# A sixteen-expert loop with its experts ranked by token count and narrower gate and up products for the smaller ones

## The reference, cut to what matters

```python
gprob = softmax(x @ w_rg + b_rg);  gp, gidx = top_k(gprob, 1)
elog_sel = (x @ w_re + b_re) of group gidx
ep, eidx = top_k(softmax(elog_sel), 2);  ep = ep / sum(ep)
combine = sum(one_hot(gidx * 4 + eidx, 16) * (gp * ep))
for wg, wu, wd, c in experts:                 # 1024x512, 1024x512, 512x1024
    acc += c[:, None] * ((silu(x @ wg) * (x @ wu)) @ wd)
y = rmsnorm(x + acc, final_g)
```

## Time and profile before

| what | us |
|---|---|
| median of 3 runs | 878.69 |
| the same, lowest and highest | 877.14, 885.36 |
| span of the profiled execution | 877.9 |
| start of the barrier's end between b2_all and b3_all, in the span | 427.3 |
| start of the first expert's first product | 431.9 |
| start of the second step | 460.8 |
| length of an undisturbed step | 26.84 |

### The profile page before, as it was taken

How to read it: one execution, slowest core, us unless ns; L and a number is a source line. 1 busy time by engine, 2 the same in 40 slices (tenths; PEclk the granted TensorE clock), 3 DMA queues, 4 the chain that set the end, 5 groups by cost and what they waited for, 6 DMA issues and landing times.

```text
span 877.9 us, 15841 instructions
## 1 busy us (share of the span) xinstructions
PE 845.3 (96%) x5828; PEld 749.4 (85%) x5828; DVE 526.8 (60%) x1237; ACT 383.5 (44%) x734; POOL 244.6 (28%) x272
## 2 busy tenths in 40 slices
PE   6999999999999999998899999999999999999993
PEld 5989879999988787775789988889988999888992
DVE  5537424657778435557585676656666656766573
ACT  7545303656367425544334434344343444433442
POOL 1000000000000110002045654447545555445472
PEclk9999999999999999999599999999999999999997
DMA  9121001102222182336188889978899887898871
GB/s 291 43 97 47 2 0 49 49 1 56 49 96 96 59 274 91 150 145 216 60 275 290 300 304 325 306 271 310 291 310 324 307 288 278 290 360 295 286 256 50
DMA packets 118505, 166.56 MB, mean 190 GB/s; under 512 B 17012, under 2 KB 95928, under 8 KB 118469
## 3 DMA queue, kind: packets, MB, share of 16 engines
q1 hardware_dynamic: 103109, 135.48, 45.7%
q0 software_dynamic: 15360, 30.59, 10.2%
HBM read 146.84 MB, written 41.17 MB: 214 GB/s over the span
## 4 chain that ended last, share of the span: by engine, by line
PE 47%; another core or an unknown queue 1%; ACT 1%; issue 1%; DVE 0%; POOL 0%; ACTq 0%; POOLq 0%
PE bank L1912 31%; PE bank L1922 4%; PE bank L1933 3%; PE bank L1924 3%; PE bank L1923 3%; PE bank L1900 2%; PE bank L1893 1%; ACT split L2012 1%; POOL out L1820 0%; PE bank L1905 0%; DVE wdlo L2116 0%; PE bank L1939 0%; DVE x L2188 0%; ACT hs L2014 0%
## 5 line engine op out<-in xcount | busy, mean ns | idle before, releaser
L1912 PE MATMUL bank<-big,ring 128*128 128x160 f32 x2048 | 286.1, 301 | 0.1
L1912 PEld LDWEIGHTS bank<-big,ring 128*128 128x128 f32 x2048 | 281.9, 191 | 1.4
L1836 POOL TENSOR_TENSOR hold_at<-ident 128x1 f32<-128x1 f32 x63 | 53.1, 842 | 175.3 <-DVE lists L2083 128.4
L2116 DVE TENSOR_TENSOR wdlo<-wdn,split 128x1024 fp32r<-128x1024 f32 x64 | 76.7, 1219 | 0.0
L2008 ACT ACTIVATE sg<-bank 128x160 f32<-128x160 f32 x64 | 19.5, 304 | 109.7 <-PE bank L1912 95.4
L2012 ACT CAST split<-wdn 128x1024 fp32r<-128x1024 f32 x64 | 64.9, 1039 | 0.0
L502 PE MATMUL bank<-split,ring_r 128*128 128x384 f32 (+1 forms) x192 | 64.4, 336 | 0.1
L504 PE MATMUL bank<-split,ring_r 128*128 128x384 f32 (+1 forms) x192 | 61.7, 321 | 0.0
L2111 DVE TENSOR_TENSOR hs<-hid,hs 128x128 fp32r<-128x128 f32 x64 | 18.9, 295 | 57.3 <-ACT hs L2014 46.8
L1922 PE MATMUL bank<-split,hs 128*128 128x512 f32 x128 | 52.6, 411 | 0.0
L1399 PE MATMUL bank<-split,ring_r 128*128 128x512 f32 (+1 forms) x128 | 51.7, 404 | 0.3 <-PEq L1191 0.3
(11 more groups left out here) (390 smaller groups left out, 1788.4 us busy)
## 6 DMA issues: line engine op xcount, KB each, us to landing
wdn<-in_w_down SPq DMA_DIRECT2D x32, 1024.0 KB
ring<-in_w_gate SPq DMA_DIRECT2D x32, 1024.0 KB, 5.4
ring<-in_w_up SPq DMA_DIRECT2D x32, 1024.0 KB
ring<-in_w_in SPq DMA_DIRECT2D x8, 1024.0 KB, 5.9
x<-in_x_prompt SPq DMA_DIRECT2D x8, 512.0 KB, 6.1
h_rows<-h SPq DMA_DIRECT2D x8, 512.0 KB, 2.6
sums<-x SPq DMA_DIRECT2D x8, 512.0 KB, 3.6
v<-in_x_prompt SPq DMA_DIRECT2D x4, 512.0 KB, 5.4
```

Source lines behind the costliest of these rows:

```text
L1836: nc.gpsimd.tensor_tensor(hold_at[:], ident[:, 0:1], ident[:, 1:2], ALU.add).then_inc(e_hold, 1)
L1912: x = nc.tensor.matmul(bank[f % 2][:, side * 256:side * 256 + W], ring[:, u, k, c0:c0 + P], xT[:, k, :], start=k == 0, stop=k == KC - 1)
L2116: nc.vector.tensor_tensor(wdlo[:, k, :], wdn[:, k // 2, (k % 2) * D:(k % 2 + 1) * D], wdhi[:, k, :].bitcast(F32), ALU.subtract).then_inc(e ...
```

## The change

The weights' layout is not touched: before and after, gate and up are read in halves of 256 columns, runs of 1 KB. What changes:

- `order_experts`, new, on VectorE at the start of the first step (before, nothing stood there but the lists of step 0): expert 0 stays first, the other 15 are ranked by count, the smallest first. It writes the experts' order (`ids`), how much narrower than 160 the place of each expert is (`shift`), the number of steps (`steps`), and part 5 of the table, and raises the rank of tokens beyond the narrow width to the second round's. The counting of steps in b2_all (three operations and three more for `steps` and `once`), and GpSimd's making of part 5, go.
- Gate and up products are 132 columns wide in steps 1 to 6, 144 in steps 7 to 12, 160 in steps 0 and 13 to 15 (`WIDTHS`); TensorE's loop becomes three. Everything else stays at 160.
- Each engine reads the number of steps later: TensorE within step 0 behind f=1, ScalarE and VectorE behind step 0, GpSimd behind its first fetches. In every step SyncE and VectorE read the expert's number from `ids`.
- Within step 0, TensorE's list product moves from behind f=0 to behind f=1, and VectorE's third table from behind f=1 to behind f=2.
- Results have a list of their own, `lists_out`. GpSimd no longer waits for the results at the end of its pass; VectorE waits for the sums sent (e_sum) before it writes `lists_now`, and for the results of the step before (e_out) before it writes `lists_out`. At the end GpSimd waits once more, with a register load between.

```diff
+WIDTHS = [(1, 132), (7, 144), (13, W)]
...
-        link(nc.vector.tensor_reduce(mxc[:, 0:1], bank[6][:, 0:NE], axis=AX.X, op=ALU.max))
-        link(nc.vector.tensor_scalar(rlim[:, 0:ROUNDS], rlim[:, 0:ROUNDS], mxc[:, 0:1], float(NE), ALU.is_lt, ALU.mult))
-        link(nc.vector.tensor_reduce(mxc[:, 1:2], rlim[:, 0:ROUNDS], axis=AX.X, op=ALU.add))
+        nc.vector.tensor_copy(order.counts, bank[6][:, 0:NE])
...
+    def expert(eng, i):
+        return eng.value_load(ids[0:1, bass.ds(i, 1)], min_val=0, max_val=NE - 1)
+
     def count(eng):
+        eng.wait_ge(e_steps, 1)
         return eng.value_load(steps[0:1, 0:1], min_val=NE, max_val=NE * ROUNDS)
...
             pool.wait_ge(e_otl, i + 1)
+            pool.wait_ge(e_to, i + 1)
             hold()
             send_results(e_out)
-            pool.wait_ge(e_out, i * 64 + 64)
-            pool.sem_inc(e_free, 1)
...
         pool.wait_ge(e_fin, 64)
+        pool.wait_ge(e_out, last_step(pool) * 64)
...
-                x = nc.tensor.matmul(bank[f % 2][:, side * 256:side * 256 + W],
-                                     ring[:, u, k, c0:c0 + P], xT[:, k, :],
+                x = nc.tensor.matmul(bank[f % 2][:, side * 256:side * 256 + w],
+                                     ring[:, u, k, c0:c0 + P], xT[:, k, 0:w],
...
-                if first and f == 0:
+                if first and f == 1:
+                    ends.extend((count(pe), last_step(pe)))
                     pe.wait_ge(e_oh, 2)
                     pe.wait_ge(e_idx, 1)
                     indices(facts)
...
-        with pe.Fori(1, n - 1) as i:
-            step(i, False, False)
-        step(m, False, True)
+        for j, (a, w) in enumerate(WIDTHS):
+            with pe.Fori(a, WIDTHS[j + 1][0] if j + 1 < len(WIDTHS) else n - 1) as i:
+                step(i, False, False, w)
+        step(m, False, True, W)
...
+        def order_experts():
...
+            link(nc.vector.tensor_tensor(compared[:], key[:].unsqueeze(1).broadcast_to(all3), key[:].unsqueeze(2).broadcast_to(all3),
+                                         ALU.is_lt))
+            link(nc.vector.tensor_reduce(place[:], compared[:], axis=AX.X, op=ALU.add))
...
         def step(i, first, last):
             if first:
-                first_lists()
+                second = second_table()
+            if not last:
+                e = expert(dve, (i + 3) % NE)
             for f in range(4):
...
                 if first and f == 0:
-                    next_lists()
-                if first and f == 1:
+                    first_two_lists(second)
+                if first and f == 2:
                     third_table()
...
-            dve.wait_ge(e_free, i + 1)
+            if not first:
+                dve.wait_ge(e_sum, i * 32)
...
+            def results_gone():
+
+                if not first:
+                    dve.wait_ge(e_out, i * 64)
+                nc.vector.tensor_copy(lists_out[:], lists_now[:, 2:4, :]).then_inc(e_to, 1)
```

More of the change, by code:

```diff
@@ L73, in __init__ @@
         self.s1, self.s2, self.gp, self.w1 = take(TT), take(TT), take(TT), take(TT)
+class Order:
+    def __init__(self, big):
+        self.counts = big[:, 3712:3712 + NE]
+        self.both = big[:, 3728:3728 + 4 * TT].rearrange("p (t j) -> p t j", t=TT)
 class Samples:
@@ L1195, in b2_all @@
 def b2_all(nc, A, O, S0, Sp, s_w, samples, halves, sb, sem, e_w, wdn, bank, ident, onesf, eps_c, uT, gT, ring, x1, x_rows, h2_dram,
-           sums_dram, rank_m, table, iota_w, steps, once, weighing, rows_0):
+           sums_dram, rank_m, table, iota_w, order, weighing, rows_0):
     c2 = ExitStack()
@@ L1216, in b2_all @@
     wr = picks.rearrange("p a t e -> p (a t e)")[:, 0:KC * SB].rearrange("p (k c) -> p k c", k=KC)
-    later = sb("later", [P, TT, 4], ctx=c2)
-    both = sb("both", [P, TT, 4], ctx=c2)
+    both = order.both
     Mb = sb("Mb", [P, TT, NE], BF16, ctx=c2)
@@ L1753, in b3_all @@
     e_oh, e_ix, e_idx = rows_0.e_oh, sem("e_ix"), sem("e_idx")
-    e_free = sem("e_free")
+    e_to = sem("e_to")
     e_far, e_next, e_now = sem("e_far"), sem("e_next"), sem("e_now")
     e_hold = sem("e_hold")
+    e_sort, e_order, e_steps = sem("e_sort"), sem("e_order"), sem("e_steps")
+    compared = sb("compared", [P, NE, NE], ctx=c3)
+    within = sb("within", [P, NE, 4], ctx=c3)
+    earlier = sb("earlier", [P, TT, NE, 4], ctx=c3)
+    most = sb("most", [P, 2], ctx=c3)
+    limits = sb("limits", [P, ROUNDS], ctx=c3)
+    key, place, shift, part = [sb(x, [P, NE], ctx=c3) for x in ("key", "place", "shift", "part")]
+    ids = sb("ids", [1, NE], I32, ctx=c3)
     e_rk = sem("e_rk")
@@ L1817, in rows_old, with send_part @@
             fetch(old2[:], expert_rows(sums_dram), lists_next, 1, e_old)
-        def send_part(kind, which, dst, rows, part, signal):
+        def send_part(lst, which, dst, rows, part, signal):
             nc.gpsimd.indirect_dma_start(
@@ L1849, in _ @@
         rows_old()
+        n = count(pool)
         with pool.Fori(0, n - 1) as i:
@@ L1940, in left_sums, with step @@
                              start=True, stop=True).then_inc(e_ms, 1)
-        def step(i, first, last):
+        def step(i, first, last, w):
             pe.wait_ge(e_xe, i * 3 + 3)
@@ L1974, in step @@
                     if last and (h, k) == (1, 1):
-                        pe.wait_ge(e_sql, n)
+                        pe.wait_ge(e_sql, ends[0])
                         left_sums()
-        n = count(pe)
-        m = last_step(pe)
         pe.wait_ge(e_xg, 16)
@@ L2037, in step @@
                 left_root()
-        with act.Fori(0, n - 1) as i:
+        step(0, False)
+        n = count(act)
+        m = last_step(act)
+        with act.Fori(1, n - 1) as i:
             step(i, False)
@@ L2231, in _ @@
         step(0, True, False)
+        n = count(dve)
+        m = last_step(dve)
         with dve.Fori(1, n - 1) as i:
```

143 lines of the change are left out of this document (90 added, 53 removed).

## The result

The kernel after the change takes 855.6 us (median of 4 runs, 854.3 to 856.3); the kernel before, run beside it, 877.95 (877.1 to 885.4). The ratio is 0.974, with an interval of 0.972 to 0.976. The profiled execution has a span of 852.5 us against 877.9. The forecast was 857.5.

What follows compares the result with a forecast made beforehand. TensorE's gate and up products were taken to bound the kernel. 877.9 - 25.0 (narrow columns) + 3.1 (steps 0 and 1) + 0.7 (end) = 856.7, with the median 0.8 higher: 857.5 us, range 852 to 867.

Steps and rivals of the forecast that it cites:

- Gain a step: TensorE's gate and up products: a step of 132 columns gains 2.57 us, one of 144 gains 1.60.
- the other bound of the same step: Gate and up products: 3.07 us gained at 132 columns and 1.75 at 144 if time went wholly with the columns.
- The new wait: TensorE's left down product waits 0.25 us for hid of f=3 in steps of 132, none at 144.
- The order of the deadlines: Narrow steps: hid of f=3 is late first, by 0.25 us at 132; hid of f=0, next, holds by 0.6 us.
- "e_free's going saves nothing else": Dropping VectorE's e_free wait saves nothing beyond its 0.79 us, which stood behind full cover of TensorE.
- Rival 2: VectorE late in every narrow step: load 0.5 more, new waits 0.8, over 0.6 of room; 863.5 us, chance 0.14.
- Step 0: Ranking on VectorE takes 8.7 us; left down product at 455.7 instead of 453.23, so 2.5 us later.
- Rival 1: TensorE's clock falls in step 0, between f=3's end and the left down product; 2.5 us, 860.0, chance 0.18.
- Step 1: Three loads between ot and hid of f=0 on VectorE make TensorE 0.6 us later.
- The end: One register load behind the last results, not hidden, costs 0.7 us.
- Rivals 3 to 5: Transfers bound narrow steps (865, chance 0.10); weights at the slowest rate (924, 0.03); second round of 16 steps (1290, 0.01).

Runs made afterwards that it cites:

- columns_96: Kernel after the change with gate and up products of 96 columns in steps 1 to 12, products of columns beyond left out; 850.2 us in one run.
- old_wait: Kernel after the change, narrow products kept, but results sent from lists_now again and VectorE waiting for e_free; 901.3 us, ratio 1.026.
- loads_early: Kernel after the change with VectorE's two loads of the number of steps moved into its waits for ScalarE; 853.5 us.
- rank_early: Kernel after the change with the first eight operations of the ranking at the end of b2_all; 857.1 us.
- all_wide: Kernel after the change with all gate and up products at 160 columns; 880.3 us, ratio 1.003.
- wide_old_wait: Kernel after the change with all gate and up products at 160 columns, results from lists_now and the e_free wait back; 882.4 us, ratio 1.005.
- low_parts: Kernel after the change with wdlo k=3 and ScalarE's copy for it behind silu and hid of f=3 instead of behind f=2; 858.0 us.
- apart_64: Kernel before the change with 64 unused bytes a partition ahead of hs and wdlo, nothing else; 878.1 us, ratio 1.000.

## Why the prediction was right, and where not

The forecast was 857.5 and the result 855.6, with the mechanism forecast: columns off the products that TensorE's time consists of. Term by term:

- **Gain a step.** Spacing was put at 115.0 and 124.5 ns by interpolation to the 111.9 ns of the 128 column row. Measured: 112.5 to 114.4, and 123.6. That row stands on the floor which columns_96 shows, so the line through it was too flat; the other bound of the same step, time going wholly with the columns, was the true one down to 132. Columns gained 1.71 us in steps of 144 (25.01 for 26.72) and 2.76 in steps of 132 (23.96 for 26.72), where 1.60 and 2.57 were forecast: 1.8 us over twelve steps.
- **The new wait** of 0.25 us ahead of the left down product in steps of 132, and none in those of 144: it came where forecast, and about half as long, 0.12 by the windows. The order of the deadlines was right too: hid of f=0 held in steady steps, with the register load showing 0.70 us instead of 0.3.
- **"e_free's going saves nothing else"** failed: with the old wait the narrow kernel takes 901, so its going is worth 45 us. The forecast did not suffer, since the change has the new list. What failed is the method: the wait's price was read at the step length of before, where GpSimd's round just fits. Rival 2 asked what the new waits cost; the length of the old round was never added up.
- **Step 0.** The ranking took 8.8 us (8.7 forecast), hid of f=0 came at 441.6 (440.8), the left down product at 457.02 (455.7). Of TensorE's wait for the lists 1.4 us stood in the working (441.7 to 443.1); it was 2.5, and what it did to the clock was missing.
- **Rival 1, the clock,** came true at another place and cost less than its price. The kernel with 96 columns runs the same step 0 without the fall: from the list product to the left down product it takes 456.62 - 444.80 = 11.8 us there, 457.02 - 443.75 = 13.3 in after. So 1.4 us, against 2.5; in old_wait, with half clock for nearly 7 us, it takes 14.5, and the price is 2.7. That is the cost at the left down product. Whether the whole time has it is not shown, for behind it columns_96 waited 3.60 us, and after did not. The wait for the lists in columns_96 was even longer (3.0 us) than in the six profiles with the fall (2.4 to 2.9), so its length alone does not decide. The Trainium skill (TensorE: Matmul & The Clock Gate, "HAM oscillation") says that idle gaps between bursts of matmuls put the array back to half rate; those six profiles agree, and that of columns_96 does not.
- **Step 1**: 0.6 forecast; 25.22 - 23.96 = 1.3 measured, 1.2 of it by the loads (loads_early).
- **The end**: 0.7 forecast, 0.1 measured. GpSimd's load stood at 846.9 to 847.4, under the landing of the last results, which e_fin waits for anyway.
- **Rivals 3 to 5** did not come: shares of 0.94 to 0.96 without a wait, one round of 16 steps.
- **Not in the sum**: 0.12 us a step (1.8 in all) from the place of the buffers, and the two long steps of the profile of before (2.0).

The sum had -25.0 for the columns and +3.8 for the rest, -21.2; the spans differ by -25.4. Of the 4.2 between, 1.8 are the columns, 1.8 the buffers and 2.0 the long steps, and 1.4 go the other way (0.9 at the barrier, 0.4 in step 0, 0.7 in step 1, less 0.6 at the end). So the hit within 2 us is luck in part: it hides errors of that size in single terms. The spans also differ by more than the medians do (25.4 against 22.4). In each of the runs of after the time stands 1.8 us over the span of the same execution, and its profiled execution was the fastest of the four, so its median stands 3.1 us over the profiled span, where 0.8 was assumed; the profile of before has the two long steps. Against the 22.4 of the medians the sum of 21.2 is 1.2 short.

## What to carry to other kernels

A wait that costs nothing today belongs to a closed round: add up the round, and compare it with the step that the change will leave, before you call it free. Take a spacing from rows at several sizes, and ask whether the smallest lies on a floor set by something else. When an early piece of the chain is moved away, look for the transfer that was issued to land just in time for the old chain.

## What the runs showed of the hardware that was not expected

- f32 products with weights of their own at 160, 144, 132 and 96 columns are 137.0, 123.6, 112.5 to 114.4 and 110.6 to 113 ns apart: proportional to the columns (0.857 ns) down to about 130, then a floor.
- 16 bytes of unused memory a partition ahead of hs and wdlo shorten each step of the kernel before from 26.84 to 26.72 us, by its 24 main down products (0.2275 us apart for 0.2333); 64 bytes don't, and 16 + 64 in rank_early don't either (0.234).
- In step 0, about an idle stretch of 2.4 to 2.9 us, TensorE's granted clock went from full to half in after, all_wide, old_wait, wide_old_wait, loads_early and low_parts, for 3 to 7 us; with 3.0 us of idling in columns_96 it did not.
- The last results of a step, scattered by GpSimd while weights are loaded, took 7.7 us to land in one step of apart_64, and `lists_now` could be written 6.1 us after their issue in old_wait.
